# The slots of each pair's second expert ranked in reverse within every group of 16 partitions

## The reference, cut to what matters

```python
g_sel = jnp.argmax(softmax(x @ wg + bg))            # 1 of 4 groups
top_v, top_i = lax.top_k(fine[g_sel], 2)            # 2 of its 8 experts
w_fine = softmax(top_v) * p_sel
y = sum over the two experts of w * (silu(x @ w_gate[e]) * (x @ w_up[e])) @ w_down[e]
x = x + g2 * y
```

## Time and profile before

| | |
|---|---|
| median of three runs | 632.15 us (632.01 to 633.56) |
| the profiled execution | 631.55 us |
| its span, first to last instruction | 629.6 us |
| PE busy | 593.3 us, 94% |
| DMA, all 16 engines | 176.23 MB, mean 280 GB/s |
| granted TensorE clock | 0.992 of full speed |

### The profile page before, as it was taken

The page is one execution under the profiler, slowest core; times in us unless marked ns, Lnnn a source line. Parts: engine busy times, 40 slices in busy tenths (PEclk is TensorE's granted clock), DMA queues, the critical chain, the costliest instruction groups (busy, mean ns, idle before and its releaser), DMA issues.

```text
span 629.6 us, 9459 instructions
## 1 busy us (share of the span) xinstructions
PE 593.3 (94%) x3309; PEld 331.4 (53%) x3310; DVE 352.3 (56%) x788; ACT 177.5 (28%) x369; POOL 94.6 (15%) x131
## 2 busy tenths in 40 slices
PE   4989999999998999999999889999999999689797
PEld 2544555555565676645555445555555555355453
DVE  2736898765664888655666873343424334313337
ACT  4203887601144787731111101101110110011110
POOL 4000011122161000000000111212122121201200
PEclk9999999999999999999999999999999999989999
DMA  8999843330029629529114959999999999999876
GB/s 318 375 370 361 318 156 138 140 133 2 0 83 280 249 92 264 238 102 398 67 68 161 382 188 392 417 419 416 420 420 410 420 417 421 419 421 416 360 280 263
DMA packets 48273, 176.23 MB, mean 280 GB/s; under 512 B 10988, under 2 KB 18168, under 8 KB 34544
## 3 DMA queue, kind: packets, MB, share of 16 engines
q1 hardware_dynamic: 36992, 154.86, 63.0%
q0 software_dynamic: 6688, 15.58, 7.1%
q10 hardware_dynamic: 4560, 5.35, 2.4%
HBM read 163.31 MB, written 21.14 MB: 293 GB/s over the span
## 4 chain that ended last, share of the span: by engine, by line
PE 67%; DMA 15%; SPq 7%; DVE 6%; issue 2%; ACT 1%; ACTq 1%; POOL 1%; DVEq 0%; POOLq 0%
PE ps L1757 16%; PE ps L1574 11%; PE ps L1773 7%; PE ps L1490 7%; PE ps L1502 6%; DMA expert_w<-exp_w_up 5%; PE ps L1612 4%; PE ps L1639 4%; DMA gate_w<-lru_wx 3%; PE ps L1621 3%; DMA w_mod_ring<-w_mod 2%; SPq L329 2%; SPq L358 2%; PE ps L1465 2%; PE ps L1725 2%
## 5 line engine op out<-in xcount | busy, mean ns | idle before, releaser
L1757 PE MATMUL ps<-expert_w,hT_mixT 128*64 128x256 f32 x1120 | 137.1, 395 | 11.9 <-DMA expert_w<-exp_w_up 11.6
L1757 PEld LDWEIGHTS ps<-expert_w,hT_mixT 128*64 128x64 f32 x1120 | 84.8, 137 | 67.6 <-issue 23.0
L1490 PE MATMUL ps<-hT_mixT,w 128*128 128x128 f32 (+1 forms) x256 | 72.6, 437 | 1.2 <-DVE hT_mixT L918 1.2
L1574 PE MATMUL ps<-w,hT_mixT 128*128 128x512 f32 x160 | 71.9, 597 | 0.0
L1773 PE MATMUL ps<-expert_w,w 128*64 128x512 f32 x280 | 65.8, 598 | 0.0
L741 ACT ACTIVATE w<-ps 128x128 f32<-128x128 f32 x36 | 10.0, 278 | 194.4 <-PE ps L1757 194.4
L1304 DVE SCALAR_TENSOR_TENSOR w<-w,ps 128x128 f32<-128x128 f32 x36 | 10.4, 288 | 88.0 <-ACT w L741 88.0
L1490 PEld LDWEIGHTS ps<-hT_mixT,w 128*128 128x128 f32 x256 | 38.9, 191 | 35.8 <-issue 32.6
L1502 PE MATMUL ps<-w_qkv,hT_mixT 128*128 128x512 f32 (+1 forms) x160 | 53.2, 488 | 0.2 <-DVE v_tok L1006 0.2
L1322 DVE TENSOR_TENSOR w<-ps,w 128x1024 f32<-128x1024 f32 x17 | 20.8, 1225 | 56.5 <-PE ps L1773 56.5
L1574 PEld LDWEIGHTS ps<-w,hT_mixT 128*128 128x128 f32 x160 | 29.1, 191 | 29.9 <-issue 29.7
(11 more groups left out here) (289 smaller groups left out, 763.6 us busy)
## 6 DMA issues: line engine op xcount, KB each, us to landing
expert_w<-exp_w_down SPq DMA_DIRECT2D x31, 1024.0 KB, 18.5
expert_w<-exp_w_gate SPq DMA_DIRECT2D x29, 1024.0 KB
expert_w<-exp_w_up SPq DMA_DIRECT2D x29, 1024.0 KB
w_mod_ring<-w_mod SPq DMA_DIRECT2D x14, 1024.0 KB, 6.5
y_rows<-zero_rows POOLq DMA_DIRECT2D x10, 512.0 KB, 9.4
expert_w<-y_rows SPq DMA_DIRECT2D x10, 512.0 KB, 8.3
recurrence<-w_mod SPq DMA_DIRECT2D x8, 512.0 KB, 9.7
w<-w_in SPq DMA_DIRECT2D x4, 1024.0 KB, 16.9
```

What stands on the lines that cost most here:

```text
L1490: ins = pe.matmul(ps[:, bank, 0:n], w1v[:, c, m * P:(m + 1) * P], HM[:, c, lo:lo + n], start=(c == 0), stop=(c == DC - 1))
L1574: ins = pe.matmul(ps[:, 2 * (t % 2) + half, :], HM[:, c, t * P:(t + 1) * P], w1v[:, c, half * 512:(half + 1) * 512], start=(c == 0), stop= ...
L1757: ins = pe.matmul(ps[r, 2 + k, 0:2 * P].rearrange("p (k f) -> p k f", k=2), xT[:, c, r], gate_up(i)[:, :, c, k:FF:FC], start=(c == 0), sto ...
```

## The change

One table of the host is different. Columns 0 to 63 of `slot` keep their values. Columns 64 to 127 held the ranks 0 to 63 (plus 1/4) in order; now each group of 16 columns holds its 16 ranks in reverse: slot 64 has rank 15, slot 79 rank 0, slot 80 rank 31, and so on. So a second expert with 18 rows fills slots 64 to 79 as before, and its rows 16 and 17 lie in slots 95 and 94 where they lay in 80 and 81. The instructions of all engines are the same, word for word and in the same order.

```diff
-            "slot": np.arange(P) % SLOTS + np.arange(P) // SLOTS / 4}[name] for name, _ in TABLE]).astype(f), (P, 1))),
+            "slot": np.where(np.arange(P) < SLOTS, np.arange(P), np.arange(P) % SLOTS // 16 * 16 + 15 - np.arange(P) % 16)
+            + np.arange(P) // SLOTS / 4}[name] for name, _ in TABLE]).astype(f), (P, 1))),
```

## The result

The changed kernel takes 634.35 us, the median of 22 runs (632.23 to 636.39); the kernel before, run beside it as often, 632.00 us. The ratio over all runs is 1.0028, its interval 1.0015 to 1.0042: 1.8 us slower, between 0.9 and 2.7 (the two medians alone differ by 2.35). The difference is real; its middle still lies within the 0.3% that the prediction calls no change. A second set of runs gave 1.0033 (1.0016 to 1.0051).

A forecast was written before the change was run, and what follows sets the result against it. The prediction took the DMA refill stream to bound the kernel from 533 to 596 us. First gather, refill stream, last scatter and reload each added 0, so 631.55 us profiled and 632.1 as median, range 630.5 to 634.2.

The forecast's parts named there:

- What bounds the kernel: DMA refill stream bounds from 533 to 596 us; PE waits four times for gate/up weights, 11.6 us in all.
- Nothing added or removed, no cost on the compute engines: Whole kernel: no instruction, DMA, byte or wait changes; cost on PE, DVE, ACT, POOL, SP 0.
- Division (a): Gathers and scatters: each half on its own eight engines, four neighbouring slots each, round twice; fullest engine 206 rows before and after.
- modulo 16: Rival (b), balance: slots fall on engines modulo 16, fullest 178 to 153 rows, 3.9 us less, 628.2; 6%.
- eights in a row: Division (c) of gather and scatter slots: eight neighbouring slots to each engine, 248 rows on the fullest before and after.
- the shared paths: Rival: engines of both halves share a way in pairs, 400 to 354 rows, 3.6 us less, 628.5; 4%.
- The price of a row, 0.156 us: DMA stream: a 4,096-byte row on one engine at 26.2 GB/s takes 0.156 us; upper bound 0.188.
- The loads change places, and no load changes: Refill stream under (a): engines 8 and 11, 9 and 10, 12 and 15, 13 and 14 swap; 0 rows, 0 us.
- The rival "slower": DMA engines: one that gains rows, 11 or 15, is slower by itself and becomes last; at worst 639.9 us; 7%.
- 12 to 18 rows were unexplained: Weight landings at 596 and 552: rows (a) leaves unexplained, 12 of 218 and 18 of 180; used against a slow engine.
- Engine 15: Slow-engine case: it goes from 102 to 152 rows; if already tied with the last, 7.8 us more, 639.9.
- The sign by PE's waits: PE's gate/up waits: 11.6 us within 1 expected; under 8 means (b) or shared paths, 13 or more a slow engine.

The follow-up runs named there:

- the piled table: Second expert's ranks piled eight to an engine, 240 rows on the fullest, against the kernel before: 642.62 us, ratio 1.0146.
- the even table: Ranks of both halves dealt out back and forth over the engines, 156 rows on the fullest, against the kernel before: 628.30 us, ratio 0.9933.
- control: No change of the table: the kernel before with its ranks written by a function; 631.54 us, ratio 0.9985.

## Why the prediction was wrong, and where it was right

**What bounds the kernel: right.** The four waits stand at the same places; the last step starts as much later (1.29 us) as the span is longer (1.3), and the tables with 240 and 156 rows on the fullest engine moved landing and time together.

**Nothing added or removed, no cost on the compute engines: right.** Same instructions, packets and bytes; late windows at 416 to 420 GB/s, first gather 3.99 us.

**Division (a): right, and now shown.** The reversal within fours leaves all as it was, the piled table makes the first gather 1 us longer, and the even table the stream 5 us shorter, where modulo 16 has it 3 longer and eights in a row have it 1.2 shorter. Modulo 16 (628.2) and the shared paths (628.5) would also have made the change faster, and are out. The Trainium skill ("DMA: Bandwidth & Descriptors", section "The descriptor swizzle") states the division for a 1 MiB transfer over 128 partitions; these runs agree with it for gathers and scatters of rows.

**The price of a row, 0.156 us: right in the mean only.** The piled table gave 7.2 us for 34 rows (0.21 each), the even table 5.0 for 50 (0.10), and between the two 84 rows are 12.2 us (0.145). The lags of the engines would explain both in part: 0.5 of the 1.9 us too much by engine 9's lag, the 2.8 too little by engine 14's.

**"The loads change places, and no load changes", so 0 us: this step failed.** The rows are 206 before and after, and the sum took engines for interchangeable. Engine 11 with 206 rows lands 1.8 to 2.5 us later than engine 8 with 206. That is the term of the sum that I put at 0; I had set aside "some ten rows (1.6 us) by which engines that change places could differ" for the range alone, and the 634.35 us lie just above its end of 634.2.

**The rival "slower" was right in kind, and its dismissal wrong.** I had written for engine 11 that any handicap counts, up to 7.2 us, and gave the rival 7% because 12 to 18 rows were unexplained at 552 and at 596 alike, while a slow engine would fall further behind. Three faults. The lag isn't a rate, so a constant rest doesn't speak against it. The rest isn't constant either: the 162 rows at 552 are gathers 1 to 14 and scatters 0 to 12, but gather 15 starts at 542.8 and scatter 13 at 548.1, both before the landing at 551.83; with the gather the fullest engine has 166 rows and with both 174, so 14 or 6 rows are unexplained there and 12 at 596. And PE's wait shows the engine that lands last and no other: engine 11, with 46 rows less, could hide 7.2 us. By division (a) the fullest engine is 0 until about 550 (154 rows at 533), and engine 8 only from about 568 on, so what I built on said something of engines 0 and 8 at most. The trace of before had more to give: its last additions at 596 are at 596.00, 595.43, 594.01 and 593.67 (control 596.09, 595.01, 594.12, 593.72; in fours 595.92, 595.09, 594.06, 593.81). They are too close for one engine to have made two of them, if one engine's part of a transfer takes 2.50 us as the prediction estimates. By rows the four fullest engines (8, 0, 9, 10) would end at 596.0, 594.1, 593.5 and 591.6, so the second addition is 0.8 to 1.3 us later than rows allow against the last, and the fourth 2.0 to 2.3. The additions have no names, but some engines lagged behind engine 8 in the kernel before already, by up to 2 us or more, and to put engines as equal could be seen to be wrong. A change that hands the bound from the one engine known to be good enough to one never seen at the bound can't be priced at 0 from both sides; the bound below was near 0, the bound above 7.2.

**Engine 15: rightly doubted.** The Trainium skill ("DMA: Bandwidth & Descriptors", section "Latency and other measured facts") calls engines 7 and 15 usually slower. Here 15 lands 1.8 us after engine 8, as 9, 10 and 11 do, and 14 is later, 2.7 us. The 639.9 us of that case did not come near; with all 206 rows on engine 15 the kernel took 633.69.

**The sign by PE's waits: half right.** "If they grow to 13 or more, a slow engine took rows": they grew to 13.4 us. But the same change in its second trace has 12.9, and the exchange of 8 and 11 alone 12.6, beside 11.6 before and 10.6 in the control. The landings, counted from the first issue, tell it apart; the sum of PE's waits also holds what PE lost or gained before them.

## What to carry to other kernels

Where one transfer is split over 16 engines, and each completion waits for all, count the rows on the fullest engine before anything else: dealing the ranks out back and forth over the groups of four took 4 us off a tuned kernel by a host table alone. A wait shows only the engine that lands last; a permutation of equal loads need not be free, because an engine that had cover may have a lag that never showed. How near the others are, the last additions to the semaphore tell, though without names: look at them before you call engines equal. When PE's waits differ by a microsecond, compare the landings from the first issue of the stream, which here repeated to 0.3 us for the table of the kernel before, but not for the three other tables that were traced twice (0.9 to 2.8 us apart at the worst mark): trace a table more than once.

## What the runs showed of the hardware that was not expected

- With another engine than 8 as the fullest at the same 206 rows, the stream's landing at 596 us came 0.7 to 2.7 us later: engine 12 by 0.7, 13 by 1.3, 10 by 1.6, 9 by 1.7 and 2.3, 15 by 1.8, 11 by 1.8 to 2.5, 14 by 2.7. Only engines 9 and 11 were traced more than once, and whether engine or partitions lag is open.
- Where these lags change, they change in steps of 0.9 to 1.6 us (9, 10 and 11), and don't grow steadily. That 16 KB packets of the instruction queue make them (1.06 us each, and mostly 0.80 instead of 0.31 for the packet behind) fits the steps of engines 9 and 10 in size and place, and isn't shown: no row names the engine, one step of 0.7 us has no such packet, and the packet didn't move in the repetition.
- The order of the rows within an engine's share of a gather makes no difference: 0.9986 against a control of 0.9985.
